# Mask, negated scores and running minimum of a 768-column softmax tile in one VectorE operation; attention scale moved into the query norm's weights

## What is computed

```
q = rmsnorm(q, qn_g);  k = rmsnorm(k, kn_g)
q = apply_rope(q, ang) * HEAD_DIM ** -0.5        # memory heads: the scale without rope
s = q @ k.T                                      # dilated heads: -inf outside the window
m = max(s, axis=-1);  p = exp(s - m);  den = sum(p)
o = (p / den) @ v
```

## Time and profile before

| | us |
|---|---|
| median of 3 runs (3617.0 to 3618.53) | 3617.51 |
| the profiled execution | 3618.54 |
| its span | 3616.7 |
| TensorE busy | 3454.8 (96%) |
| VectorE busy | 1579.7 (44%) |
| ScalarE busy | 1329.2 (37%) |
| GpSimd busy | 1412.0 (39%) |
| mean granted TensorE clock | 0.982 |

### The profile page before, as it was taken

One profiled execution on the slowest core, in us unless ns is written; L12 is line 12 of the kernel. 1 busy time (PEld: TensorE's weight loads), 2 busy tenths in 40 slices (PEclk: granted clock), 3 DMA queues, 4 the chain that ended last, 5 costly groups with the idle time before them and its releaser, 6 DMA issues.

```text
span 3616.7 us, 46305 instructions
## 1 busy us (share of the span) xinstructions
PE 3454.8 (96%) x16866; PEld 2870.5 (79%) x16866; DVE 1579.7 (44%) x2569; ACT 1329.2 (37%) x2048; POOL 1412.0 (39%) x1040
## 2 busy tenths in 40 slices
PE   8999998899999999999899999989998999998898
PEld 7888876888888888887688888878787877887677
DVE  2221456452215422145655220563686388345633
ACT  3222435442224422243544222463343244444343
POOL 5544432055544454443304554443332433352222
PEclk9999999999999999999999999989999999999999
DMA  4232221022223222222102232322211211231111
GB/s 155 93 99 94 82 70 41 1 94 94 97 93 99 77 98 99 93 82 70 53 1 80 95 99 93 107 80 79 74 61 41 82 65 59 70 128 59 41 53 59
DMA packets 76662, 281.14 MB, mean 78 GB/s; under 512 B 8512, under 2 KB 8640, under 8 KB 76128
## 3 DMA queue, kind: packets, MB, share of 16 engines
q1 hardware_dynamic: 75600, 274.66, 23.1%
q10 hardware_dynamic: 912, 4.39, 0.3%
HBM read 276.92 MB, written 2.10 MB: 77 GB/s over the span
## 4 chain that ended last, share of the span: by engine, by line
PE 87%; DVE 8%; ACT 3%; issue 2%; DMA 0%; DVEq 0%; ACTq 0%; SPq 0%
PE ps L1729 15%; PE ps L1731 15%; PE ps L1730 15%; PE ps L1801 3%; PE ps L1803 3%; PE ps L1802 3%; PE ps L2263 3%; PE ps L2249 2%; PE ps L1840 2%; PE ps L1838 2%; PE ps L1839 2%; PE ps L2189 1%; PE ps L2310 1%; PE ps L2190 1%; PE ps L2191 1%
## 5 line engine op out<-in xcount | busy, mean ns | idle before, releaser
L526 POOL TENSOR_TENSOR w_lo<-raw,w_hi 128x512 fp32r<-128x512 f32 x1028 | 1400.4, 1385 | 2181.3 <-ACT w_hi L577 2181.2
L1729 PE MATMUL ps<-x_hi,w_hi 128*128 128x512 f32 x2560 | 1049.4, 410 | 4.6 <-issue 4.6
L1731 PE MATMUL ps<-x_hi,w_lo 128*128 128x512 f32 x2560 | 999.9, 391 | 0.0
L1730 PE MATMUL ps<-x_lo,w_hi 128*128 128x512 f32 x2560 | 999.3, 390 | 0.0
L577 ACT ACTIVATE w_hi<-raw 128x1024 fp32r<-128x1024 f32 x514 | 542.2, 1057 | 1083.0 <-PE ps L1731 596.2
L1729 PEld LDWEIGHTS ps<-x_hi,w_hi 128*128 128x128 f32 x2560 | 483.1, 189 | 125.8 <-issue 29.5
L1730 PEld LDWEIGHTS ps<-x_lo,w_hi 128*128 128x128 f32 x2560 | 482.6, 189 | 118.8 <-issue 22.4
L1731 PEld LDWEIGHTS ps<-x_hi,w_lo 128*128 128x128 f32 x2560 | 481.6, 188 | 102.3
L1186 DVE TENSOR_TENSOR T<-T,ps 128x512 f32<-128x512 f32 x88 | 60.5, 688 | 661.0 <-PE ps L1731 651.7
L698 ACT ACTIVATE T<-ps 128x512 f32<-128x512 f32 x88 | 52.6, 598 | 360.0 <-PE ps L1731 354.5
L1838 PE MATMUL ps<-h_hi,w_hi 128*128 128x512 f32 (+1 forms) x440 | 153.2, 348 | 0.0
(11 more groups left out here) (326 smaller groups left out, 5331.9 us busy)
## 6 DMA issues: line engine op xcount, KB each, us to landing
raw<-in_weights SPq DMA_DIRECT2D x514, 512.0 KB, 3.3
Y<-in_x_t SPq DMA_DIRECT2D x1, 2048.0 KB, 7.9
mem<-in_mem_t ACTq DMA_DIRECT2D x2, 1024.0 KB, 6.6
out_t<-Y SPq DMA_DIRECT2D x8, 256.0 KB, 2.2
ple_p<-in_p_t ACTq DMA_DIRECT2D x2, 512.0 KB, 5.3
mat<-in_mats SPq DMA_DIRECT2D x1, 768.0 KB, 11.6
masks<-in_masks ACTq DMA_DIRECT2D x1, 576.0 KB, 8.2
rope<-in_rope_b ACTq DMA_DIRECT2D x1, 512.0 KB, 6.7
```

Source lines behind the costliest of these rows:

```text
L526: ins = pool.tensor_tensor(g.wl[:, k, part], g.raw[:, k, part], g.wh[:, k, part], ALU.subtract)
L1729: mm(out, wh[:, c], xh[:, kc, :], start=kc == 0, stop=False)
L1730: mm(out, wh[:, c], xl[:, kc, :], start=False, stop=False)
L1731: ins = mm(out, wl[:, c], xh[:, kc, :], start=False, stop=kc == DC - 1)
```

## The change

In kind "a", the two mask additions, the maximum and the product with -SCALE become one operation over 768 columns, `tensor_tensor_reduce`: it writes -(scores + mask) into T, and the minimum of these values, which is minus the maximum, into `nb`. The masks are laid out anew so that the 768 columns of a tile lie side by side (3072 instead of 2304 columns of two bytes, with the tensors behind them moved by a KiB). In kinds "b" and "mem" the maximum is negated by the reduction itself, and the product goes. The scale goes into the norm weights of the queries: three small operations at the start of the program multiply them, and signal `consts_done`; each application of a norm also waits for that. The exponential then has the scale -1 (kind "a") or 1 in place of SCALE.

```diff
@@ build
-        g.MASK = over("masks", (P, 2304), BF16, 72)
+        g.MASK = over("masks", (P, NT, 768), BF16, 72)
...
@@ act_program, group
-            fn(buf, src, ACT.Exp, scale=SCALE, bias=g.small[:, 9, e % 2:e % 2 + 1],
+            fn(buf, src, ACT.Exp, scale=-1.0 if kind == "a" else 1.0, bias=g.small[:, 9, e % 2:e % 2 + 1],
...
@@ dve_program, qk_apply
         dve.wait_ge(s.qrs_done, r + 1)
+        dve.wait_ge(s.consts_done, 7)
...
@@ dve_program, group
             dve.wait_ge(s.s_mm, e + 1)
             if kind == "a":
                 dve.wait_ge(s.pt_mm, e - 1)
-                link(v.tensor_tensor(buf[:, 0:S], flat[:, 4 * S:5 * S], g.MASK[:, c * S:(c + 1) * S], ALU.add))
-                link(v.tensor_tensor(buf[:, S:768], flat[:, 5 * S:5 * S + 256], g.MASK[:, 4 * S:4 * S + 256], ALU.add))
-            link(v.tensor_reduce(nb, buf if kind == "a" else ps[:, 4 + e % 2, 0:width], AX.X, ALU.max))
-            v.tensor_scalar(nb, nb, -SCALE, None, ALU.mult).then_inc(s.smax_done, 1)
+                v.tensor_tensor_reduce(buf, flat[:, 4 * S:4 * S + width], g.MASK[:, c, :], -1.0, -2 * MASKED, ALU.add,
+                                       ALU.min, nb).then_inc(s.smax_done, 1)
+            else:
+                v.tensor_reduce(nb, ps[:, 4 + e % 2, 0:width], AX.X, ALU.max, negate=True).then_inc(s.smax_done, 1)
...
@@ dve_program, start
     dve.wait_ge(s.const_landed, 32)
+    for name in ("mem_q", "qn_a", "qn_b"):
+        q = g.vec[:, VEC[name][0]:VEC[name][0] + VEC[name][1]]
+        v.tensor_scalar(q, q, SCALE, None, ALU.mult).then_inc(s.consts_done, 1)
```

More of the change, by code:

```diff
@@ L179, in build @@
         g.O = over("o", (P, 12, S), F32, 48)
-        g.MASK = over("masks", (P, 2304), BF16, 72)
[L181 to L184, removed]
+        g.MASK = over("masks", (P, NT, 768), BF16, 72)
+        g.ROPE = over("rope", (P, 2, S), F32, 78)
+        g.RS = over("rstd", (P, 2, S), F32, 82)
+        g.MT = over("mem_tmp", (P, 4, N_MEM), F32, 82)
+        g.TR = over("rope_partner", (P, S), F32, 86)
         g.OH = over("o_hi", (P, 12, S), F32R, 0)
@@ L721, in arena @@
                 act.dma_start(g.MEM[:, :, :], T["mem_t"]).then_inc(s.arena_landed, 16)
-                act.dma_start(g.MASK[:, :], T["masks"]).then_inc(s.arena_landed, 16)
+                act.dma_start(g.MASK[:, :, :], T["masks"]).then_inc(s.arena_landed, 16)
                 act.dma_start(g.ROPE[0:32, :, :], T["rope_a"]).then_inc(s.arena_landed, 16)
@@ L885, in gate @@
             fn(out, out, ACT.Exp, scale=-1.0).then_inc(s.sig_done, 1)
-        act.wait_ge(s.consts_done, 4)
+        act.wait_ge(s.consts_done, 7)
         norm(n, eps_ln, [u0 + 12, u0 + 13] + ([u0 + 14, u0 + 15] if l else []), gate)
@@ L2470, in window_masks @@
     i = np.arange(P)[:, None]
-    out = np.zeros((P, 2304), np.float32)
+    out = np.zeros((P, NT, 768), np.float32)
     for c in range(NT):
-        out[:, c * S:(c + 1) * S] = np.where(abs(c + 4 * i - np.arange(S)[None]) <= 64, 0, MASKED)
+        out[:, c, 0:S] = np.where(abs(c + 4 * i - np.arange(S)[None]) <= 64, 0, MASKED)
     j = np.arange(P)[None]
-    out[:, 2048:2176] = np.where(abs(i - j) <= 64, 0, MASKED)
-    out[:, 2176:2304] = np.where((i - j) % 4 == 0, 0, MASKED)
+    out[:, :, S:S + P] = np.where(abs(i - j) <= 64, 0, MASKED)[:, None]
+    out[:, :, S + P:] = np.where((i - j) % 4 == 0, 0, MASKED)[:, None]
     return out.astype(mybir.dt.np(BF16))
```

## The result

The changed kernel takes 3599.09 us (median of 5 runs, 3596.83 to 3599.86) against 3618.46 of the kernel before on the same chip (5 runs, 3617.0 to 3619.93). The ratio is 0.9946, with a 95% interval of 0.9933 to 0.9959: faster by 19.4 us. I had forecast 13.0 us less and a range that began at 3600.0, so the sign holds, and so does the mechanism of the waits, while the time lies 0.9 us outside the range: the prediction left out most of what the clock gave. The profiled execution took 3599.86 us with a span of 3597.7, so the spans differ by 19.0 us, and these are what the traces have to account for.

A forecast was written before the change was run, and what follows sets the result against it. TensorE, working in 96% of the span, was taken as the bound, so only its waits counted: 6.0 + 0.6 + 2.2 + 2.7 + 1.5 = 13.0 us off the profiled 3618.5, median 3604.5 us, range 3600.0 to 3614.5.

The forecast's parts named there:

- five waits of 1.6: Layer A, transposes waiting for the scaled tile: five waits each 1.2 us shorter, 6.0 us.
- the 5.33 wait with the clock behind it: First value unit of A's second half: wait ends 1.2 us earlier, half lost to a slow stretch staying put, 0.6 us.
- the 3.48 wait, rope included: Before a head's first scores: 1.2 us from the tile, 1.0 from rope operations starting ahead of GpSimd, 2.2 us.
- clock behind it: Behind the 3.48 us wait: clock of 0.62 returns to 1.00 once 1.3 us of wait are left, 2.7 us.
- layer B, waits and clock: Layer B: eight waits and the 6.0 us one each 0.18 us shorter, a little at half clock, 1.5 us.
- The operations beside the bound: Mask additions' replacement, three small start operations, larger masks and tiles TensorE doesn't wait for: covered by TensorE's products, cost nothing.
- The value that was chosen between the bounds: Fused layer A tile: 1.12 us, between bounds of 1.03 and 2.05, in place of 2.32; saves 1.2 us per tile.
- Rival 4: More than forecast: another slow stretch goes, or layer B rope operations slip past GpSimd; some 4.5 us, 3600 us, chance 0.12.
- Rival 1: Clock behind the 3.48 us wait stays low: 9.2 us saved, 3608.3 us, chance 0.20.
- Rival 2: Fused operation goes at half rate or twice over its columns, 1.9 to 2.05 us: 3613.7 us, chance 0.15.
- rival 3: Fused operation not built-in and costly to change to; slower above 2.32 us per tile: 3625.1 us, chance 0.05.
- Rival 5: At layer A's five waits something else is late behind the tile: only 3 us come, 3614.5 us, chance 0.03.

The follow-up runs named there:

- the doses: The changed kernel with one or two unused maxima behind each fused operation of layer A, ahead of the signal: 3607.48, 3612.87 and 3615.86 us.
- dose_768_256: The changed kernel with two unused maxima, of 768 and 256 columns, behind each fused operation of layer A, ahead of the signal: 3615.86 us.
- fill2_before: The kernel before with unused matrix products that fit into seven of TensorE's waits (5, 6, and 2 or 3 in each of five): 3607.89 us.
- dose_768: The changed kernel with one unused maximum of 768 columns behind each fused operation of layer A, ahead of the signal: 3612.87 us.
- a_only: The kernel before with the fused operation in layer A alone, the scale in its factor; layer B and memory tiles as before: 3605.12 us.
- b_only: The changed kernel with layer A's fused operation replaced by two additions, a maximum and a negation; layer B and memory edits kept: 3618.28 us.
- dose_256: The changed kernel with one unused maximum of 256 columns behind each fused operation of layer A, ahead of the signal: 3607.48 us.
- the three fill2 kernels: The kernel before, the changed kernel, and the kernel with layer A's fusion alone, each with fitting unused products in seven waits: 3607.89, 3592.43 and 3595.91 us.
- again: The changed kernel measured once more, unedited: 3598.68 us.
- fill2_after: The changed kernel with unused matrix products that fit into seven of TensorE's waits (4, 6, and 2 or 3 in each of five): 3592.43 us.

## Why the prediction was right and wrong

The forecast was 13.0 us, and 19.4 came. Term by term, against the table of stretches:

| term | forecast | measured |
|---|---|---|
| five waits of 1.6 | 6.0 | 6.8 |
| the 5.33 wait with the clock behind it | 0.6 | 1.6 |
| the 3.48 wait, rope included | 2.2 | 2.2 |
| clock behind it | 2.7 | 2.0 |
| clock behind the 2.62 wait | 0 | 1.6 |
| layer B, waits and clock | 1.5 | 5.5 |
| first block and rest | 0 | -0.7 |
| sum | 13.0 | 19.0 |

**Right.** TensorE waits at few places, and what counts there is how early the exponential may start: the doses carried each 0.5 us to the wait of the transposes, and stretch A back to 829.0 us. The operations beside the bound came at nothing, as far as the equality of dose_768_256 and before in stretch A, to 1 us, can show it. The new operation takes the time of one pass (0.94 against 0.95 taken). The rope slips past GpSimd with the three durations that were drawn up, and the clock behind that wait is back at 1.00.

**The value that was chosen between the bounds.** I took 1.12 us for the fused tile, and it is 0.97, below even the lower bound, which stood there as 1.03 with "a read-out that lies nearly beside it". The choice was made by L1565, 0.15 for one column, a different operation. The read-out adds 0.01 us to the operation. The choice cost 0.15 us at each of five places, 0.8 us together, and part of the next term.

**The 5.33 wait.** The step that failed is "if that slow stretch stays where it is, TensorE gets 1.2 us more of it". The slow part behind the wait was 3.9 us of work before (clock 0.73) and is 3.5 now (0.76): it moved along with the end of the wait. So all 1.36 us counted, and not half.

**Layer B is the step that broke the range.** The term was 1.5 us: nine waits by 0.18, with "a little of it at half clock". It measured 5.5. The waits gave 1.0 us and not 1.6, since the last got longer; the other 4.4 are the clock, which the term held to be a small loss. The clock is low in stretches all over the query units, and the earlier trace rows had it: 0.91 over 140 us are 25 us at 1.2 GHz. Some 3 us of that are the end of B's long wait, where nothing is lost; the 22 us of the window above, 11 us lost, are the largest sum of clock in the profile. I had priced the clock behind two waits of layer A to a tenth of a us and left this row as a count of busy time. Rival 4 named one place of it, B's long wait, with 2 us; the five waits of 2.4 to 3.4 us, each followed by slow products, were in no case. fill2_before shows what was at stake at these places and the 5.33 one together: 10.7 us. The change took 4.2 us of that.

**The 2.62 us wait.** The prediction had no term for the clock behind it. In the profiled pair it gave 1.6 us. The slow stretch is missing in both traces of the changed kernel and in dose_768, while six other kernels with the fused operation and this wait unfilled have it. So this part of the gain is luck as far as the runs tell; none shows why it came.

**Rival 4** was the nearest, at 3600 us: slow stretches went at two more places than forecast, behind the 2.62 us wait (1.6 us, a place it hadn't named) and in layer B. No rope operation in layer B was needed for it. **Rival 1** fell with the clock of 1.00 at 3057.00. **Rival 2** fell with 937 to 958 ns, and so did **rival 3**, whose break-even of 2.32 us dose_768_256 puts on the chip: at 2.39 us per tile, layer A is back to 829.0 us. **Rival 5** fell with the waits, which are 0.20 to 0.24 long and name the scaled tile.

**What stays open.** Why the clock behind waits of one and the same length is low in one kernel and not in the next. The wait of 2.62 us has a slow stretch behind it in before, a_only, b_only, dose_256, dose_768_256, the three fill2 kernels and the two with too many products, none in after, again and dose_768. B's long wait is 5.80 us in both b_only and after, and more is slow behind it in b_only (0.56 over the next 7 us, against 0.74). The length alone doesn't decide. Perhaps the moment at which a wait falls does, but no run here isolates that. So I can say what the clock gave (by fill2_before against fill2_after), but not forecast which slow stretch goes. Open too is whether the layer B edits give more together with layer A's than alone: the medians say 6.2 against 0.1 us, stretch B says 4.3 to 5.4 against 2.0, and the intervals allow for either.

## What to carry to other kernels

Where an engine waits for a chain of small operations, count the chain's latency at the waits that remain and not its busy time; 1.35 us from 32 tiles were worth something at seven of them. Then price the clock in every window in which it is below 1.00, by its length, before the edit's own terms: the low clock behind seven waits of 2.4 to 6 us cost this kernel 10.7 us, over half of what the change brought. Where a wait can't be removed, products that nothing reads hold the clock, if their number is sized from one measured product (0.87 us here) and stays below the wait: 5 in the wait of 5.33 us left 1.0 us idle and the clock at 1.00, while the kernels with 13 in a wait of 4.0 to 5.3 us, and with too many in the others, got slower.

## What the runs showed of the hardware

- The fused operation with a running minimum takes 937 to 958 ns for 768 columns, with the scores from PSUM and a two-byte mask from SBUF, as long as the plain maximum over 768 (0.95) and less than the two additions (1.11). Its read-out of 71 to 84 ns begins 70 ns ahead of the operation's end.
- GpSimd that starts in the middle of a VectorE operation doesn't stretch it: L1539 at 3054.21 took 0.68 us though GpSimd began at 3054.53; the next took 1.64.
- Filling a wait can be worth more than shortening it: products without a use took 9.3 us from stretch B (235.8 to 226.5), the whole change 5.2, and 10.7 us from the kernel before, with its own work unchanged.
- A tile that becomes ready sooner by 0.18 us can leave TensorE a wait longer by 0.41 (2.43 in a_only, 2.84 in b_only), where the clock ahead of it is 1.00 in place of 0.85.
